# Triangular systems inverted from 16x16 blocks, in place of seven doubling levels

## The reference, cut to what matters

```python
amat = jnp.where(strict, bc[..., :, None] * decay * jnp.einsum('bhntd,bhnsd->bhnts', kc, kc), 0.0)
rhs = jnp.concatenate([bc[..., None] * vc, (bc * jnp.exp(g))[..., None] * kc], axis=-1)
sol = lax.linalg.triangular_solve(amat + jnp.eye(c, dtype=jnp.float32), rhs,
                                  left_side=True, lower=True, unit_diagonal=True)
```

```python
sa = jnp.einsum('bhvk,bhk->bhv', s, a_)
s = s * w_[:, :, None, :] + sa[..., None] * b_[:, :, None, :] + v_[..., None] * k_[:, :, None, :]
```

## Time and profile before

| | |
|---|---|
| three runs | 2271.18, 2281.61, 2282.57 us; median 2281.61 |
| span of the profiled execution | 2267.6 us |
| median and fastest run beside that span | 14.0 and 3.6 us above it |
| busy time over the span | PE 2018.1 us (89%), PEld 1799.9, DVE 878.4, ACT 605.7, POOL 532.4 |
| starts of tiles 0 to 7 and of the sample tile (L1774) | 606.5, 679.3, 763.5, 849.6, 934.1, 1020.2, 1112.5, 1196.9, 1284.5 us |

### The profile page before, as it was taken

How to read it: one execution, slowest core, us unless ns; L and a number is a source line. 1 busy time by engine, 2 the same in 40 slices (tenths; PEclk the granted TensorE clock), 3 DMA queues, 4 the chain that set the end, 5 groups by cost and what they waited for, 6 DMA issues and landing times. The chain is left out here.

```text
span 2267.6 us, 33912 instructions
## 1 busy us (share of the span) xinstructions
PE 2018.1 (89%) x13531; PEld 1799.9 (79%) x13531; DVE 878.4 (39%) x1457; ACT 605.7 (27%) x1144; POOL 532.4 (23%) x445
## 2 busy tenths in 40 slices
PE   3999949999599999999999888689999997899986
PEld 2799949888598888888888766479999997677764
DVE  4355524665435535535436433330011001444432
ACT  4344432333233223222233212232111110211101
POOL 2322021110255335334344310121112110100000
PEclk6999979999799999998999987699999998688887
DMA  4122130321431201201203201342212211623214
GB/s 128 31 78 77 50 110 27 98 90 57 151 101 43 71 29 51 69 28 51 67 17 83 56 13 33 87 134 87 86 40 79 75 59 37 190 81 92 88 47 43
DMA packets 192188, 160.55 MB, mean 71 GB/s; under 512 B 34562, under 2 KB 174059, under 8 KB 192088
## 3 DMA queue, kind: packets, MB, share of 16 engines
q1 hardware_dynamic: 192088, 159.12, 24.0%
HBM read 103.96 MB, written 55.14 MB: 70 GB/s over the span
## 5 line engine op out<-in xcount | busy, mean ns | idle before, releaser
L1318 POOL TENSOR_TENSOR c_m<-c_sc,c_lev 128x512 f32<-128x512 f32 (+1 forms) x118 | 155.1, 1325 | 46.6 <-DVE c_sc L1614 43.6
L1846 PEld LDWEIGHTS c_bank<-c_inv,c_m 128*128 128x128 f32 (+1 forms) x1200 | 149.8, 197 | 8.9 <-issue 8.7
L1846 PE MATMUL c_bank<-c_inv,c_m 128*128 128x64 f32 (+1 forms) x1200 | 154.8, 275 | 0.5
L1318 POOL TENSOR_TENSOR c_m<-c_nt,c_lev 128x512 f32<-128x512 f32 (+1 forms) x59 | 79.4, 1346 | 261.7 <-PE c_bank L1846 131.7
L1656 DVE TENSOR_TENSOR c_inv<-c_inv,c_bank 128x256 f32<-128x256 f32 (+1 forms) x126 | 51.0, 414 | 213.5 <-PE c_bank L1858 213.5
L1754 PE MATMUL c_bank<-c_wo,c_ot 128*128 128x512 f32 (+1 forms) x288 | 132.3, 615 | 0.5 <-ACT c_invt L1371 0.5
L2290 DVE SCALAR_TENSOR_TENSOR e_t<-e_t,e_bank 128x512 f32<-128x512 f32 (+1 forms) x20 | 12.7, 633 | 289.7 <-ACT e_t L2243 289.7
L85 PE MATMUL e_bank<-e_wp0h,e_xh 128*128 128x256 f32 x432 | 123.1, 285 | 1.8 <-issue 1.8
L87 PE MATMUL e_bank<-e_wp0h,e_xl 128*128 128x256 f32 x432 | 123.0, 285 | 0.0
L86 PE MATMUL e_bank<-e_wp0l,e_xh 128*128 128x256 f32 x432 | 122.9, 285 | 0.0
L85 PE MATMUL e_bank<-e_wp1h,e_xh 128*128 128x256 f32 x432 | 122.3, 283 | 0.0
(11 more groups left out here) (562 smaller groups left out, 5181.9 us busy)
## 6 DMA issues: line engine op xcount, KB each, us to landing
e_w<-in_w_in_dram SPq DMA_DIRECT2D x16, 1024.0 KB, 6.6
b_w<-in_w_in_dram SPq DMA_DIRECT2D x17, 512.0 KB, 6.4
scratch_rw<-b_x SPq DMA_DIRECT2D x16, 544.0 KB, 2.7
a_w<-in_w_in_dram SPq DMA_DIRECT2D x16, 512.0 KB, 5.8
c_rw<-scratch_rw SPq DMA_DIRECT2D x32, 256.0 KB, 3.0
scratch_qkv<-a_o SPq DMA_DIRECT2D x12, 544.0 KB, 4.5
e_xs<-scratch_xnT SPq DMA_DIRECT2D x8, 544.0 KB, 4.2
scratch_ql<-e_qb SPq DMA_DIRECT2D x8, 544.0 KB, 2.9
```

The source lines that it names most:

```text
L1318: pool.tensor_tensor(M[u][0:T, :, 0:T], src, bc(lev[0:T, l:l + 1, 0:T], [T, 4, T]), ALU.mult).then_inc(ev(f"m{u}"), 1)
L1846: mm = pe.matmul(packed(2 * u, l, T, T)[:, k], M[u][0:T, k, 0:T], half(X[u][0:T, k, :], l, T, 0), start=True, stop=True)
```

## The change

The seven levels are replaced in all prompt tiles by a base of 16x16 blocks and three levels above it.

- **Base.** SP stores `NT` and the triangles in `SC` to a DRAM scratch (`S.nd`) and reads back the 16x16 blocks on their diagonals, 96 blocks as 96 partitions of 256 numbers, in two transfers of 48 (`spread_out`). DVE inverts them (`invert`): a copy of the identity, then seven steps of two small operations on the two 8x8 blocks of each, and four larger ones that join them. Each operation waits for the one before it.
- **The way back.** SP writes the inverses to a second scratch (`S.ub`) in two transfers and reads them as `UC`, 128 partitions with twelve heads of 32 (`gather`). DVE transposes `UC` in 32x32 blocks into `XC`.
- **Three levels.** `lower_parts` on PE goes from 16 to 32, 64 and 128 by two sets of products a level: y4 and z4 (48 products each, 16 columns, weights of 32 columns and fewer), y5 (24) and z5 (36), of 32 columns, y6 and z6 (12 each, 64 columns). ACT and DVE carry each set to SBUF; after level 4 DVE transposes `UC` again. POOL copies the pieces into the inverses `XN` and `XT` (`place`), and its 21 masking operations are gone, with DVE's L1623 and the ACT copies of the levels.
- **The projection.** The first half of the previous tile's output projection goes ahead of y4, right behind that tile's transposes; the eight products of the second half are placed between the sets, 2, 2, 1, 1, 1 and 1 of them.
- **The rest of the order.** On DVE the scores are masked earlier (four ahead of `NT`, four behind `attn`), and `end_sums`, `end_gate` and `end_rows` of the previous tile go ahead of `Wr`, `RH` and the base; `end_add` goes behind the state's `NVd`. On SP the store of the blocks opens a tile, and `gather` stands behind the loads of q, k, v, a, b, k of the next tile and behind `load_z`. Banks of PSUM are dealt out anew.
- **Once.** `UC` is zeroed and written over `S.ub`; this store is queued on SP behind the load of `wo`, and SP waits for it before tile 0.
- **Sample tile.** Its blocks of 8 need the base alone; both projection halves run on PE in the meantime.

```diff
+                def spread_out(i, T):
+                    n = i + 1
+                    nd = S.nd[:, 0:P * P].rearrange("h (s t) -> s h t", t=P)
+                    sp.wait_ge(ev("nt_a"), n)
+                    alone(sp, K)
+                    sp.dma_start(nd[0:T, 0:AH, 0:T], NT[0:T, :, 0:T]).then_inc(ev("n_out"), 16)
+                    sp.wait_ge(ev("sc"), 8 * n)
+                    alone(sp, K)
+                    sp.dma_start(nd[0:T, AH:NH, 0:T], SC[0:T, :, 1, 0:T]).then_inc(ev("n_out"), 16)
+                    sp.wait_ge(ev("n_out"), 32 * n)
+                    alone(sp, K)
+                    blocks = S.nd.rearrange("h (q r) -> (h q) r", q=8)[:, 0:16 * P].rearrange("(k e) (s t) -> e k s t", e=2, t=P)
+                    for e in range(2):
+                        sp.dma_start(grid(base[48 * e:48 * e + 48, 0:256]), blocks[e][:, :, 0:16]).then_inc(ev("ba"), 16)
+                def gather(i):
+                    n = i + 1
+                    sp.wait_ge(ev("ub"), n)
+                    alone(sp, K)
+                    rows = S.ub.rearrange("h (g e s) c -> e (h g) s c", g=4, e=2)
+                    for e in range(2):
+                        sp.dma_start(rows[e][:, :, 16 * e:16 * e + 16], grid(base[48 * e:48 * e + 48, 256:512])).then_inc(ev("u_out"), 16)
+                    sp.wait_ge(ev("u_out"), 32 * n)
+                    alone(sp, K)
+                    sp.dma_start(UC[:, :, :], S.ub.rearrange("h s c -> s h c")).then_inc(ev("uc"), 16)
...
 
                     n, c = i + 1, i * P
+                    spread_out(i, P)
...
                         alone(sp, K)
                         load_z(c, P)
+                    gather(i)
+                    if not (isinstance(i, int) and i == 0):
...
                 load_x(0, P)
                 sp.dma_start(wo[:, :, :], w_block(w_out, 0, D)).then_inc(ev("ld_wo"), 16)
+                sp.wait_ge(ev("cleared"), 1)
+                sp.dma_start(S.ub.rearrange("h s c -> s h c"), UC[:, :, :]).then_inc(ev("ub_zero"), 16)
+                sp.wait_ge(ev("ub_zero"), 16)
...
-                            src = NT[0:T, :, 0:T] if u == 0 else SC[0:T, 4 * (u - 1):4 * u, 1, 0:T]
-                            pool.tensor_tensor(M[u][0:T, :, 0:T], src, bc(lev[0:T, l:l + 1, 0:T], [T, 4, T]),
-                                               ALU.mult).then_inc(ev(f"m{u}"), 1)
...
+                    pool.wait_ge(ev("gw"), n)
+                    if T == P:
+                        pool.wait_ge(ev("xc"), 2 * n)
+                        alone(pool, K)
+                        for b in range(2):
+                            pool.tensor_copy(XN[sub(b), :, sub(b)], XC[sub(b), :, :]).then_inc(ev("xn"), 1)
+                            pool.wait_ge(ev("xn"), 2 * i + b + 1)
+                            alone(pool, K)
+                        for k, g in enumerate((2, 3, 0, 1)):
+                            pool.tensor_copy(XT[sub(g), :, sub(g)], UC[sub(g), :, :]).then_inc(ev("xt"), 1)
+                            pool.wait_ge(ev("xt"), 4 * i + k + 1)
+                            alone(pool, K)
...
+                def invert(i):
+                    dve.wait_ge(ev("u_out"), 32 * i)
+                    dve.tensor_copy(UB, EYE).then_inc(ev("ub_eye"), 1)
+                    dve.wait_ge(ev("ba"), 32 * n)
+                    dve.wait_ge(ev("ub_eye"), n)
+                    step.start(i)
+                    A, U = eights(0), eights(256)
+                    for k in range(7, 0, -1):
+                        w = 8 - k
+                        t = TM[:, 0:2 * k * w].rearrange("p (b s t) -> p b s t", b=2, s=k)
+                        shape = [8 * NH, 2, k, w]
+                        step(dve.tensor_tensor(t, A[:, :, 0:k, k:k + 1].broadcast_to(shape), U[:, :, k:k + 1, k:8].broadcast_to(shape), ALU.mult))
+                        step(dve.tensor_tensor(U[:, :, 0:k, k:8], U[:, :, 0:k, k:8], t, ALU.subtract))
+                    cube = [8 * NH, 8, 8, 8]
+                    t = TM.rearrange("p (s t k) -> p s t k", s=8, t=8)
+                    b = BM.rearrange("p (s t) -> p s t", s=8)
+                    A, U = grid(BA), grid(UB)
+                    step(dve.tensor_tensor(t, A[:, 0:8, 8:16].rearrange("p s (a k) -> p s a k", a=1).broadcast_to(cube),
+                                           U[:, 8:16, 8:16].rearrange("p k (a t) -> p a t k", a=1).broadcast_to(cube), ALU.mult))
+                    step(dve.tensor_reduce(b, t, AX_X, ALU.add))
+                    step(dve.tensor_tensor(t, U[:, 0:8, 0:8].rearrange("p s (a k) -> p s a k", a=1).broadcast_to(cube),
+                                           b.rearrange("p k (a t) -> p a t k", a=1).broadcast_to(cube), ALU.mult))
+                    dve.tensor_reduce(U[:, 0:8, 8:16], t, AX_X, ALU.add, negate=True).then_inc(ev("ub"), 1)
+                    step.end()
...
+                    scores(range(4, 8))
+                    if last is not None:
+                        end_sums(last, P)
...
-                    for u in range(3):
-                        dve.wait_ge(ev(f"m{u}"), LEVELS * i + 1)
-                        dve.wait_ge(ev("w_mm" if u == 0 else "sa_mm"), i)
-                        dve.tensor_tensor(XT[u][0:T, :, 0:T], bc(K.ident[0:T, 0:T].rearrange("p (a c) -> p a c", a=1), [T, 4, T]),
-                                          M[u][0:T, :, 0:T], ALU.subtract).then_inc(ev(f"xt1_{u}"), 1)
...
+                    invert(i)
+                    if T == P:
+                        lower_parts(i)
...
+                def lower_parts(i, fill):
...
+                    pe.wait_ge(ev("xc"), 2 * i + 1)
+                    for h in range(NH):
+                        for g in range(4):
+                            mm = pe.matmul(bank[g][sub(g), 16 * h:16 * h + 16], nt(h, sub(g), sub(g)), XC[sub(g), h, 0:16], start=True, stop=True)
+                    mm.then_inc(ev("y4mm"), 1)
+                    fill(0, 2)
+                    pe.wait_ge(ev("y4a"), n)
+                    pe.wait_ge(ev("y4d"), n)
+                    for h in range(NH):
+                        for g in range(4):
+                            mm = pe.matmul(bank[g][32 * g:32 * g + 16, 256 + 16 * h:272 + 16 * h], Y4[sub(g), h, :], UC[sub(g), h, 16:32], start=True, stop=True)
+                    mm.then_inc(ev("z4mm"), 1)
+                    fill(2, 4)
+                    pe.wait_ge(ev("wr"), n)
+                    pe.wait_ge(ev("rh"), n)
+                    pe.wait_ge(ev("xc"), 2 * n)
+                    for h in range(NH):
+                        for p in range(2):
+                            mm = pe.matmul(bank[4 + p][sub(2 * p + 1), 32 * h:32 * h + 32], nt(h, sub(2 * p), sub(2 * p + 1)), XC[sub(2 * p), h, :], start=True, stop=True)
+                    mm.then_inc(ev("y5mm"), 1)
+                    fill(4, 5)
+                    pe.wait_ge(ev("y5a"), n)
+                    pe.wait_ge(ev("y5d"), n)
+                    for h in range(NH):
+                        c = slice(32 * h, 32 * h + 32)
+                        pe.matmul(bank[0][sub(0), c], Y5[sub(1), h, :], UC[sub(1), h, :], start=True, stop=True)
+                        pe.matmul(bank[1][sub(2), c], Y5[sub(3), h, :], UC[sub(3), h, :], start=True, stop=True)
+                        mm = pe.matmul(bank[2][sub(1), c], UC[sub(1), h, :], Y5[sub(1), h, :], start=True, stop=True)
+                    mm.then_inc(ev("z5mm"), 1)
+                    fill(5, 6)
+                    pe.wait_ge(ev("xn"), 2 * n)
+                    pe.wait_ge(ev("u5a"), n)
+                    for h in range(NH):
+                        o = bank[3][64:128, 64 * h:64 * h + 64] if h < AH else bank[4][64:128, 64 * (h - AH):64 * (h - AH) + 64]
+                        mm = pe.matmul(o, nt(h, slice(0, 64), slice(64, 128)), XN[:, h, :], start=True, stop=True)
+                    mm.then_inc(ev("y6mm"), 1)
+                    fill(6, 7)
+                    pe.wait_ge(ev("y6a"), n)
+                    pe.wait_ge(ev("y6d"), n)
+                    pe.wait_ge(ev("xt"), 4 * n)
+                    pe.wait_ge(ev("u5d"), n)
+                    for h in range(NH):
+                        o = bank[5][0:64, 64 * h:64 * h + 64] if h < AH else bank[1][0:64, 64 * (h - AH):64 * (h - AH) + 64]
+                        mm = pe.matmul(o, Y6[:, h, :], XT[64:128, h, 64:128], start=True, stop=True)
+                    mm.then_inc(ev("z6mm"), 1)
+                    fill(7, 8)
...
-                            for k in range(4):
-                                if l < LEVELS - 1:
-                                    mm = pe.matmul(packed(2 * u + 1, l, T, T)[:, k], XT[u][0:T, k, 0:T], Y[u][0:T, k, 0:T // 2], start=True, stop=True)
-                                else:
-                                    mm = pe.matmul(packed(2 * u, l, T, P // 2)[:, k], Y[u][0:T, k, 0:P // 2], half(XT[u][0:T, k, :], l, T, 1), start=True, stop=True)
-                            mm.then_inc(ev(f"zmm{u}"), 1)
```

(12 more changed lines are left out.)

417 lines of the change are left out of this document (209 added, 208 removed).

## The result

The changed kernel took 2145.35 us in the median of four runs (2138.84 to 2149.25), against 2281.95 in four runs of the kernel before: a ratio of 0.9418, with a 95% interval of 0.9388 to 0.9449. I had forecast 2244 and a range down to 2165. The direction was right; the gain was 137 us, and I had expected 38. Each of the four runs lies 1.7 to 1.8 us above the span of its own execution (2138.84 above 2137.1), so the 14.0 us that I had put between span and median as the launch is nearly all difference from run to run.

The account below looks back on a forecast made before the run. PE was taken to bound tiles 1 to 7: 37.5 + 29.4 + 13.6 = 80.5 us each, not 86.5, 42 less over seven; sample tile -9, tile 0 +13 gave 2229.6, plus 14.0 about 2244; 8-in-10 range 2165 to 2335.

Parts of the forecast that it names:

- The chain: DVE's work and the way through DRAM ahead of y4: base done at 29.1 us, y4 starting at 37.5.
- the hops: Transfer steps carrying the inverted base through DRAM, taken at 3.0 us each; 7.9 us for the way with issues.
- One sign: PE would stand idle for 8 to 12 us ahead of y4, released by DVE's transpose.
- The small products: The 360 instructions of the six sets on PE, at 29 ns for weights of 32 columns: 12.1 us a tile.
- a rival at 0.20: Lighter products: quarters of the array overlap and the fill holds the clock; a tile 71.4 us, total 2178, chance 0.20.
- The clock: PE at clock 0.50 through y4, two fill products, z4 and a little of the next: 7.8 us a tile.
- the late return: PE's clock stays at 0.50 past y4 and the first two fill products, through z4 (2.8 us more) and 0.4 beyond.
- The case of the clock down: A rival in which PE's clock stays down to the end of the stretch; chance 0.24.
- The change of shape: Twelve changes in the shape of PE's weights between sets and fill, 0.2 us each: 2.4 us a tile.
- Tile 0: The first tile, waiting for the zeroing store behind the 4 MB load: 13 us longer, ends 0 and +20.
- The sample tile: From its first inversion product to the use of the inverses, 23.5 us in place of 32.5: 9 less.
- the 7.8 of overlapping pieces: The six sets on PE at 15 ns an instruction if pieces of the array overlap: 7.8 us in all.

Follow-up runs that it names:

- e3: The changed kernel with six extra products, later overwritten, keeping PE busy ahead of y4; ratio 0.9350 to the kernel before, tiles 1 to 7 took 459.3 us.
- e1: The changed kernel with y4, z4 and z5 reordered, all heads of one 32x32 quarter of TensorE first; tiles 1 to 7 took 537.1 us.
- e2: The changed kernel with the projection's whole second half ahead of y4, nothing between the sets; ratio 0.9535 to the kernel before, tiles 1 to 7 501.6 us.

## Why the prediction was wrong, point by point

| step, in us of a tile | forecast | tile 3 after |
|---|---|---|
| `RH` done | 22.8 | 24.3 |
| base done | 29.1 | 31.2 |
| y4 starts | 37.5 | 37.5 |
| six sets | 12.1 | 7.1 |
| fill, with changes of shape and clock | 7.1 + 2.4 + 7.8 | 9.8 |
| tail | 13.6 | 13.4 |
| tile | 80.5 | 68.0 |

**The chain** was right as a whole, by two errors that cancel: DVE was 2.1 late (`RH` by 1.5, and two of the base's four wide operations took over 1.0), and the hops were shorter: 5.6 us for the way I had at 7.9. That y4 came at 37.5 to the tenth is luck. One sign failed: PE was idle for 6.0 us ahead of y4 and not 8 to 12, since the first half started at 22.8 and took 8.6, at a clock of 0.82 in the mean.

**The small products** are the first term of the sum that was mis-sized: 12.1 us forecast, 7.1 measured, or 6.6 with y4 at full clock as in e3. The price I took, 29 ns for 32 columns, is right for a quarter by itself: e1 shows 24 and 30. What failed is the step that made the width of the weights the whole price ("The width of the weights counts, not the columns") and left the overlap to a rival at 0.20. e1 shows the overlap to be worth 2.5. That rival is what came, and even it was too long, with a stretch of 20.3 where 17.0 was measured. In e1's order five tiles took 72.8 to 75.9 us and two, with the clock down, 84.2; my 80.5 lies between, and no tile took it. (For 64 columns give 65 ns from start to start and not the 58 that I wrote; the sum used 64.)

**The clock.** It fell where I said, and the cost was 2.3 us a tile (e3) and not 7.8. This is the second mis-sized term. The 7.8 us have y4, z4 and the fill around them at the low clock, and no run shows that term. In the changed kernel y4 took 0.5 us more than in e3 and the first piece of the fill 1.8 more, and that was all. I had carried the late return over from the sample tile, where 8 us of small products and waits stood behind the fall. Here the clock was back as z4 began, behind y4 (1.4 us) and one piece of the fill (3.7 us at 0.50). In five of e1's tiles too, with a y4 of 4.6 us in tile 2, it was back at about z4, so the late return was wrong with or without the overlap; the overlap made y4 short, and only without it, in e1, did the clock stay down in two tiles. The case of the clock down was real, and its place is e1 and e2. y4 started at 0.50 behind 6.0 to 6.7 us of idle time in each of tiles 1 to 7 of the changed kernel, and at 1.00 in e3, where 0.7 us and less were left of that time. In e2 the clock fell behind much shorter waits, 0.9 and 1.6 us.

**The change of shape.** From start to start, the second to sixth piece of the fill took 0.8 us more than their products at full clock, 0.17 a piece; with the first piece's, an estimate, about 1.0 in place of 2.4. What the change costs at the end of a set is in the sets' times.

**Tile 0** lost 5.6 and not 13: y4 came at 654.5 and not 659.9, with the store landed by 634.5 in place of 636.9, the sets took 16.5 in place of 21, and the tail 13.4 in place of 11.7. **The sample tile** took 60.9 us from its start to the use of its inverses in place of 70.4, a gain of 9.5 (9 forecast); with everything behind it the gain was 8.5, but that part differs by more from run to run.

In the sum: tiles 1 to 7 took 478.0 us in place of 563.5, which is 85, tile 0 is 8, and the rest of the 99 us between 2244 and 2145 is in where the median lies above the span. Sets, clock and change of shape were all too large, by 5.5, 5.5 and 1.4 us a tile. The first two I had set apart from each other, as if they could err to either side independently; the clock's term was made of the length of the sets at 0.50, so they erred together. With the 7.8 of overlapping pieces for the products, and nothing for clock and shape, a tile is 66.0 us and the sum 2142: the range should have reached that far.
